# Two-layer transformer kernel: sums in another order, opening sums in PSUM, one-column table loads

## The reference, cut to what matters

```python
h = _rmsnorm(x, g_mix[l])
p = h @ w_in[l]
c_q = _rmsnorm(p[..., :o1], g_q[l]);      q = c_q @ w_uq[l]
c_kv = _rmsnorm(p[..., o1:o2], g_kv[l]);  kv = c_kv @ w_ukv[l]
y_attn = _mla_attention(q_nope, q_rope, k_nope, k_rope, v)      # 8 heads
a, gt = jnp.split(p[..., o3:], 2, axis=-1)
u = a * jax.nn.sigmoid(gt)
u = _dwconv(u, w_dw_conv[l], b_dw_conv[l])                      # 31 taps, 512 channels
u = jax.nn.silu(_layernorm(u, g_conv_ln[l], b_conv_ln[l]))
x = x + jnp.concatenate([y_attn, u], axis=-1) @ w_o[l]
h2 = _rmsnorm(x, g_ffn[l])
z = _dwconv(h2 @ w_up[l], w_dw_ffn[l], b_dw_ffn[l])
zg, zv = jnp.split(z, 2, axis=-1)
x = x + (jax.nn.silu(zg) * zv) @ w_down[l]
```

## Time and profile before

| what | value |
|---|---|
| three executions | 2976.78, 2978.93, 2981.33 us |
| median | 2978.93 us |
| profiled execution | 2977.82 us |
| its span | 2975.9 us |
| PE busy | 2815.8 us (95%) |
| PE weight loads busy | 2305.1 us (77%) |
| POOL busy | 1761.4 us (59%) |
| DVE busy | 1719.7 us (58%) |
| ACT busy | 778.9 us (26%) |
| mean granted clock of PE | 0.975 |

### The profile page before, as it was taken

How to read it: one execution, slowest core, us unless ns; L and a number is a source line. 1 busy time by engine, 2 the same in 40 slices (tenths; PEclk the granted TensorE clock), 3 DMA queues, 4 the chain that set the end, 5 groups by cost and what they waited for, 6 DMA issues and landing times.

```text
span 2975.9 us, 36204 instructions
## 1 busy us (share of the span) xinstructions
PE 2815.8 (95%) x13018; PEld 2305.1 (77%) x13018; DVE 1719.7 (58%) x1934; ACT 778.9 (26%) x1268; POOL 1761.4 (59%) x1000
## 2 busy tenths in 40 slices
PE   6989999999989999989999989999999998899998
PEld 5777888887777888867776778888777776788886
DVE  7874566427854665265665557064666666842644
ACT  3433222103432222024555222010222222310202
POOL 5795666665975666644443448666553343566663
PEclk9999999999999999999999989999999999899999
DMA  3202222332012222321111223322221111222231
GB/s 136 70 7 79 94 97 94 106 100 78 29 53 82 94 96 99 106 79 64 64 64 43 73 68 107 99 93 98 76 93 57 57 57 50 78 99 95 96 99 57
DMA packets 66481, 237.39 MB, mean 80 GB/s; under 512 B 7265, under 2 KB 7521, under 8 KB 66337
## 3 DMA queue, kind: packets, MB, share of 16 engines
q1 hardware_dynamic: 65504, 234.00, 23.7%
q10 hardware_dynamic: 832, 1.51, 0.2%
HBM read 233.38 MB, written 2.10 MB: 79 GB/s over the span
## 4 chain that ended last, share of the span: by engine, by line
PE 78%; DVE 8%; POOL 7%; DVEq 3%; issue 2%; ACT 1%; DMA 0%; ACTq 0%; SPq 0%; POOLq 0%
PE ps L466 24%; PE ps L472 23%; PE ps L469 23%; POOL ptmp L423 3%; POOL yconv L428 3%; PE ps L1071 2%; DVE qw L2291 1%; PE ps L860 1%; DVEq L2293 1%; POOL w_lo L407 1%; PE ps L863 1%; PE ps L1107 1%; DVE xres L2185 0%; DVE root L1573 0%; PE ps L491 0%
## 5 line engine op out<-in xcount | busy, mean ns | idle before, releaser
L405 POOL TENSOR_SCALAR w_hi<-w_raw 128x1024 fp32r<-128x1024 f32 x437 | 481.5, 1102 | 1147.5 <-PE ps L466 1132.8
L407 POOL TENSOR_TENSOR w_lo<-w_raw,w_hi 128x1024 fp32r<-128x1024 f32 x437 | 1105.3, 2529 | 36.5
L466 PE MATMUL ps<-x_hi,w_hi 128*128 128x512 f32 x2024 | 817.4, 404 | 57.7 <-DVE x_lo L2177 16.3
L469 PE MATMUL ps<-x_lo,w_hi 128*128 128x512 f32 x2024 | 800.2, 395 | 0.0
L472 PE MATMUL ps<-x_hi,w_lo 128*128 128x512 f32 x2024 | 799.8, 395 | 0.0
L466 PEld LDWEIGHTS ps<-x_hi,w_hi 128*128 128x128 f32 x2024 | 387.8, 192 | 155.7 <-issue 27.3
L472 PEld LDWEIGHTS ps<-x_hi,w_lo 128*128 128x128 f32 x2024 | 387.2, 191 | 83.7
L469 PEld LDWEIGHTS ps<-x_lo,w_hi 128*128 128x128 f32 x2024 | 387.8, 192 | 82.0 <-issue 3.8
L466 PE MATMUL ps<-a_hi,w_hi 128*128 128x512 f32 x512 | 200.0, 391 | 0.0
L472 PE MATMUL ps<-a_hi,w_lo 128*128 128x512 f32 x512 | 199.2, 389 | 0.0
L469 PE MATMUL ps<-a_lo,w_hi 128*128 128x512 f32 x512 | 199.2, 389 | 0.0
(11 more groups left out here) (386 smaller groups left out, 4566.6 us busy)
## 6 DMA issues: line engine op xcount, KB each, us to landing
w_raw<-wts SPq DMA_DIRECT2D x437, 512.0 KB, 3.2
xres<-xT SPq DMA_DIRECT2D x2, 1024.0 KB, 8.9
outT<-xres SPq DMA_DIRECT2D x8, 256.0 KB, 2.0
pf<-pT ACTq DMA_DIRECT2D x2, 512.0 KB, 3.6
prm<-prm SPq DMA_DIRECT2D x1, 452.0 KB, 4.3
lev<-levels ACTq DMA_DIRECT2D x1, 384.0 KB, 3.0
wtmp<-pos SPq DMA_DIRECT2D x1, 128.0 KB, 2.8
ident<-identity SPq DMA_DIRECT2D x1, 64.0 KB, 10.7
```

The costliest lines, as they stand in the source:

```text
L405: nc.gpsimd.tensor_scalar(w_hi[:, s, :], w_raw[:, s, :], 1.0, 0.0, ALU.mult, ALU.add).then_inc(w_rounded[s], 1)
L407: nc.gpsimd.tensor_tensor(w_lo[:, s, :], w_raw[:, s, :], w_hi[:, s, :].bitcast(F32), ALU.subtract).then_inc(w_split[s], 1)
L466: mm = nc.tensor.matmul(out, whi, xhi, start=first, stop=False)
L469: mm = nc.tensor.matmul(out, whi, xlo, start=False, stop=False)
```

## The change

1. The first sums of squares are made in PSUM bank 7 instead of in `root`; the seventh add writes `root`.
2. PE's row sums and factor for x come three and four inner steps earlier in the input product; those for KV and query one tile later each.
3. DVE's add of POOL's convolution tile moves behind the last row maximum and the division of head 5; PE's `stat` moves behind scores 2 of the last head.
4. DVE issues no convolution taps between the maxima of head 0; since `conv` counts on, the later calls take them up.
5. ACT gets seven one-column activations, `table`, each of a function that is needed later, and the squares of the first convolution tile move out of the last head to behind it.

```diff
-        consts, _ = at("consts", [P, 4])
-        epsc, turn, eps2 = consts[:, 0:1], consts[:, 1:2], consts[:, 2:3]
+        consts, _ = at("consts", [P, 5])
+        epsc, turn, eps2, spare = consts[:, 0:1], consts[:, 1:2], consts[:, 2:3], consts[:, 4:5]
...
-                    if t == 3 and kt == 2:
+                    if t == 2 and kt == 6:
                         pe.wait_ge(s_id, 16)
                         row_factor(ps[4], l * 5)
...
-                    if t == 2 and kt == 4:
+                    if t == 2 and kt == 1:
                         row_stat(ps[4], l, 0)
...
-                    if t == 6:
+                    if t == 7:
                         pe.wait_ge(rstd_ready, l + 1)
                         row_stat(ps[4], l, 1, 0)
-                    if t == 7:
+                    if t == 8:
                         row_factor(ps[4], l * 5 + 1)
-                    if t == T_KR:
+                    if t == T_KR + 1:
                         pe.wait_ge(kvn_ready, l * KKV + KKV)
                         row_stat(ps[4], l, 2, 1)
-                    if t == T_KR + 1:
+                    if t == T_KR + 2:
                         row_factor(ps[4], l * 5 + 2)
...
-                stat(ps[6][:, :], l, 3)
                 for kt in range(TT):
...
+                    if kt == 2:
+                        stat(ps[6][:, :], l, 3)
...
+            def table(func):
+
+                nc.scalar.activation(spare[:, :], epsc[:, :], func)
...
+            table(ACT.Sqrt)
             for m in range(2, KD):
                 square(m, m, xres[:, m, :])
...
                 sigmoid(3)
+                table(ACT.Exp)
                 for h in range(HEADS):
...
-                            if h == HEADS - 1:
-                                conv_square(0)
...
-                for c in range(1, CT):
+                table(ACT.Sqrt)
+                for c in range(CT):
                     conv_square(c)
                 sqrt(ps[7], 3, CONV_CH, epsc[:, :])
+                table(ACT.Silu)
...
+                table(ACT.Sqrt)
...
                 sqrt(ps[4], 4, D, epsc[:, :])
+                table(ACT.Silu)
...
                 product_round(FT - 1)
+                table(ACT.Sqrt)
...
-                add_square(m, m == KD - 1, m, 0, root)
+                dve.drain()
+                dve.wait_ge(x_sq, m + 1)
+                if m == 0:
+                    V.tensor_copy(ps[7][:, :], sq[:, 0, :]).then_inc(sq_used, 1)
+                else:
+                    V.tensor_tensor(ps[7][:, :] if m < KD - 1 else root[:, :], ps[7][:, :], sq[:, m % 2, :],
+                                    ALU.add).then_inc(sq_used, 1)
+            dve.drain().then_inc(sum_ready, 1)
...
-                        conv(1)
+                        conv(1 if h else 0)
...
-                            dve.drain()
-                            dve.wait_ge(pconv_done, l + 1)
-                            V.tensor_tensor(ssum[:, :], ssum[:, :], yconv[:, POOL_CH, :], ALU.add).then_inc(sum_ready, 1)
                     conv(3)
                     if h:
                         o_part(h - 1)
+                    if h == HEADS - 2:
+                        dve.wait_ge(pconv_done, l + 1)
+                        V.tensor_tensor(ssum[:, :], ssum[:, :], yconv[:, POOL_CH, :], ALU.add).then_inc(sum_ready, 1)
```

## The result

| | before | after |
|---|---|---|
| median | 2979.23 us (4 runs) | 2960.22 us (4 runs, 2957.41 to 2963.30) |
| ratio to before | | 0.9938, 95% interval 0.9922 to 0.9953 |
| profiled execution, its span | 2977.82, 2975.9 us | 2957.41, 2955.6 us |
| PE busy | 2815.8 us | 2807.6 us |
| DVE, POOL, ACT busy | 1719.7, 1761.4, 778.9 us | 1707.9, 1759.2, 780.5 us |

The change is faster, by 19.0 us. I had said 2948.0 with a range up to 2960: the sign was right, the gain was 29.6 us on paper and 20.3 in the two spans, and the median lies just outside the range.

What follows compares the result with a forecast made beforehand. PE works nearly all the span, so gains come from its waits and half clock; POOL's chain sets attention's end. 8.5 + 3.1 + 2 x 8.7 + 2.6 - 2 x 1 = 29.6 off 2977.8: 2948.2, stated 2948.0 us, range 2938 to 2960.

Steps and rivals of the forecast that it cites:

- Opening in PSUM: Layer 0 opening: adds take 0.85 us each, sum ready at 29.2, the 3.3 us wait goes, PE 6.0 us ahead.
- KV and query a tile later: KV and query sums before attention: with the opening, 8.5 us gained up to there in layer 0, 3.1 in layer 1.
- Mixer sum: End of attention: PE no longer stands before the last head, squares' chain ends at 226.8 against 235.5; 8.7 us per layer.
- Squares behind the exponential: Mixer squares of tiles 0 and 1, moved behind the last exponential and a table load, cost nothing.
- Table loads: One-column activations take the load from in front of the root after the mixer's output; 2.6 us over both layers.
- Half clock +1 per layer: New waits ahead of attention bring half clock, partly hidden by POOL's margin; 1 us lost per layer, bounds 0 and 4.8.
- Late PE: Rival: half clock comes with the new waits, PE late in attention by the full bound; 2955.8 us, chance 0.12.
- Slow DVE along KV and query: Rival: POOL holds DVE's SBUF operations along that stretch, 2 us per layer; 2952 us, chance 0.10.
- PSUM adds: Rival: opening adds no faster in PSUM, sum still ready at 37.3, PE waits 5.4 us; 2953.6 us, chance 0.07.
- clock luck: Rival: the norm before the feed-forward keeps full clock, sparing up to 4.8 us per layer; 2938.6 us, chance 0.08.
- half clock through attention: Rival: PE at half clock for half of attention, 38.7 us per layer; 3025 us, chance 0.03 including unseen waits that size.
- PE waiting over 3 us at the column-sum matmul: Listed sign that the prediction is wrong: such a wait at the matmul behind the mixer sum, near the last head.

Runs made afterwards that it cites:

- e6: The change with KV and query row sums and factors back at their old tiles; median 2945.0 us, ratio 0.9888 to the kernel before.
- e1: The change with the mixer's squares summed in PSUM bank 6; median 2951.8 us, ratio 0.9920 to the kernel before.
- e2: The change without the one-column square root ahead of the mixer's squares; median 2958.2 us, ratio 0.9942 to the kernel before.
- e17: e14 without the seven one-column activations; median 2939.7 us, ratio 0.9870 to the kernel before.
- e14: The change with the mixer's squares summed in PSUM and KV and query sums at their old tiles; median 2932.4 us, ratio 0.9846 to the kernel before.
- e7: The change without its seven one-column activations; median 2955.3 us, ratio 0.9926 to the kernel before.
- e16: The change itself, unaltered, timed and profiled a second time; median 2958.7 us, ratio 0.9930 to the kernel before.
- e13: The change with POOL holding W_O's third weight split until the mixer's sum of squares is ready; median 2944.4 us, ratio 0.9896 to the kernel before.

## Why the prediction was right or wrong

- **Opening in PSUM: right.** Row sums at 31.93 without a wait (forecast 31.9), sum ready at 29.1 (29.2), and PE 6.3 us ahead at the end of tile 6 (59.6 against 65.94; forecast 6.0). One bound there is a slip: seven adds of 0.69 us without a gap end at 28.0, not at 28.9.
- **KV and query a tile later: times right, credit wrong.** 65.09 (65.0), though the sum was ready 6.2 us before that and not some 4, since its copy was no longer stretched; first tap 103.59 (102.9), waits of 2.23 and 4.10 us (2.1 and 4.5), query product 115.52 (114.85); 7.9 us and, in layer 1, 15.1 - 12.4 = 2.7 us, against 8.5 and 3.1. (12.4: the lead that PE has at the first product of layer 1, 652.36 before, 639.97 after.) But I compared the new place with the *old wait*, not with the wait that the old place would have once the opening is 6 us earlier and the copy of the KV squares takes 0.43 us. There is none (e6), and the step lost 12 to 15 us that the rest of the change had earned. This credit is in no term of the sum, which was worked out for the new place, so it did not move the forecast.
- **Mixer sum, "the squares' chain on DVE after that matmul (… four sums, 7.2 us with waits)": this is the step that failed.** Up to the matmul the working held (210.34; the forecast's place, in time of after, is 210.1). The 7.2 us were taken from a place where POOL was idle, and the very move brings the chain from behind POOL's four splits for W_O (the last ended at 231.3 before) to beside the third and fourth. I had used the rule (an SBUF add beside POOL is stretched, a PSUM one is not) for the opening and for the 1.52 us add, and not here. Measured: 3.3 us longer for the sums, PE's wait 3.84 for 0.30, and 6.8 us at half clock. Over the mixer and up to the feed-forward the two layers give 2.4 and 3.4 us (11.6 - 7.9 - 1.3 and 19.8 - 15.1 - 1.3) where I had 2 x 7.7: 9.6 us short, where 29.6 - 20.3 is 9.3; the small errors elsewhere cancel but for 0.3. With the step cured (e1) the 8.7 us came, in both layers.
- **Squares behind the exponential "nothing": right**, by e2.
- **Table loads 2.6 us: right in the wait** (1.92 to 0.65, 1.27 us per layer). In time e17 against e14 says 5 us by spans, with the clock, and e7 against the change says nothing; that part stays open.
- **Half clock +1 per layer: not paid in the first profile, paid in the second.** The stretch ahead of head 0 was 3.4 us in the first profile of the change, as assumed; but in the second (e16) the granted clock from 110 to 125 us was 0.66, against 0.89 in the first:

```profile
110.00:125.00 15.00, 10.76 (x34) 7.98 (x33) 11.40 (x17) 7.83 (x14) 14.63 (x11) 0.66 0.22 72
```

  In the first profile POOL's taps hid it whole; in e16 the mixer's row sums came 3.6 us later after the query product in layer 0 (110.1 us against 106.5). So this part varies between executions of one kernel, which accounts for some of the spread.
- **Rivals.** "Late PE", 2955.8, gives nearly the time of the profiled execution (2957.4) by another cause. In the first profile its half clock cost nothing ahead of attention, and the time went behind the mixer; layer 0 of e16 shows that it can happen as well. That its figure lies near the measured one is luck. Slow DVE along KV and query did not happen (waits there are as forecast). PSUM adds were not slow (0.70 us), clock luck did not come (the granted clock is still 0.52 in the 10.24 us from 272.60), and half clock through attention did not either (1.00 from 130 to 213 us). The point "PE waiting over 3 us at the column-sum matmul" of my list did not come; that it could happen one step later, at the row sums, was not on it.

## What to carry to other kernels

When a step is moved, look up what the *other* engines do at the place it comes to, and price every operation for that company; a duration from the old place holds only there. Here the chain of adds kept its 0.7 us per add beside POOL's splits only with an operand in PSUM (e1), or with POOL held for 3 us (e13). And when two edits cure the same lateness, price the second with the first already in: a step put later to avoid a wait that is gone anyway is a plain delay, and here it sat on the path that set the start of POOL's 106 us.

## What I had not expected of the hardware

- The stretch acts both ways: POOL's rounding of a weight block takes 1.04 to 1.05 us beside PSUM adds and 1.22 to 1.48 beside SBUF adds.
- The same unlucky meeting falls differently from one execution to the next: in e16 PE's wait for these sums was 2.66 us in layer 0 and 5.79 in layer 1, against 3.84 twice in the first profile. DVE's timeline of e16:

```profile
840.16 2.58 DVE L1582 TENSOR_TENSOR ssum<-ssum,sq 128x512 f32<-128x512 f32 x1 [0.17 <-issue]
842.90 1.28 DVE L1582 TENSOR_TENSOR ssum<-ssum,sq 128x512 f32<-128x512 f32 x1 [0.16 <-issue]
844.35 2.58 DVE L1582 TENSOR_TENSOR ssum<-ssum,sq 128x512 f32<-128x512 f32 x1 [0.17 <-issue]
```

- A wait that grew by 1.27 us (e17) went with 3.4 us more at half clock behind it: near such waits the price of a microsecond is not one microsecond.
